# Down weights of the experts: from the sync engine's DMA queue to ACT's, in a two-layer mixer and MoE kernel

## The reference

```python
N_EXPERTS, TOP_K, D_EXPERT = 64, 8, 256
...
    def expert_block(args):
        b_tok, b_w, e = args
        xb = xt[b_tok]
        h = jax.nn.silu(xb @ w_gate[e]) * (xb @ w_up[e])
        return (h @ w_down[e]) * b_w[:, None].astype(xt.dtype)
...
    routed = jax.ops.segment_sum(y_rows.reshape(rows, d), row_tok, num_segments=t)
    shared = (jax.nn.silu(xt @ sw_gate) * (xt @ sw_up)) @ sw_down
    return (routed + shared).reshape(bsz, s, d)
```

## Time and profile before

| | |
|---|---|
| time, 3 runs | 1300.17 us median (1300.01 to 1300.87) |
| the profiled execution | 1300.64 us, of which the span from first to last instruction is 1298.9 us |
| mean granted TensorE clock | 0.997 of full speed |
| PE busy | 1281.4 us, 99% of the span |
| DVE, ACT, POOL busy | 529.0, 190.6 and 46.6 us |
| moved by DMA | 462.33 MB, 356 GB/s over the span |
| expert loads | 128 each of gate, up and down, 1024 KB each |

### The profile page before, as it was taken

One profiled execution on the slowest core, in us unless ns is written; L12 is line 12 of the kernel. 1 busy time (PEld: TensorE's weight loads), 2 busy tenths in 40 slices (PEclk: granted clock), 3 DMA queues, 4 the chain that ended last, 5 costly groups with the idle time before them and its releaser, 6 DMA issues.

```text
span 1298.9 us, 17051 instructions
## 1 busy us (share of the span) xinstructions
PE 1281.4 (99%) x6781; PEld 695.3 (54%) x6781; DVE 529.0 (41%) x1070; ACT 190.6 (15%) x318; POOL 46.6 (4%) x76
## 2 busy tenths in 40 slices
PE   9999999999999999999999999999999999999997
PEld 7874754544445444455487757444544445544443
DVE  6785723333333333333327155333333333333324
ACT  3231201111111111111022303111111111111111
POOL 6200100000000000000010001000000000000000
PEclk9999999999999999999999999999999999999999
DMA  7865959999999999999843278799999999999992
GB/s 256 242 248 191 423 213 412 418 422 422 422 422 421 422 422 422 421 422 421 349 161 130 83 285 337 283 419 420 422 422 422 422 422 422 422 422 422 422 420 87
DMA packets 77625, 462.33 MB, mean 356 GB/s; under 512 B 9680, under 2 KB 10896, under 8 KB 27152
## 3 DMA queue, kind: packets, MB, share of 16 engines
q1 hardware_dynamic: 77584, 461.74, 87.6%
HBM read 455.36 MB, written 6.36 MB: 355 GB/s over the span
## 4 chain that ended last, share of the span: by engine, by line
PE 96%; DVE 2%; DMA 1%; ACT 0%; issue 0%; SPq 0%; ACTq 0%
PE bank L1065 34%; PE bank L1097 18%; PE bank L995 10%; PE bank L1016 9%; PE bank L622 6%; PE bank L636 4%; PE bank L968 2%; PE bank L689 2%; PE bank L703 2%; PE bank L1076 1%; PE bank L1004 1%; PE bank L1030 1%; DMA weight_ring<-in_w_in_even 1%; PE bank L800 1%; DVE h L1353 1%; PE bank L891 1%
## 5 line engine op out<-in xcount | busy, mean ns | idle before, releaser
L1097 PE MATMUL bank<-expert_weights,hiddenT 128*64 128x512 f32 x1024 | 233.8, 598 | 0.0
L1065 PE MATMUL bank<-expert_weights,hT 128*64 128x512 f32 x1024 | 225.3, 592 | 0.0
L1065 PE MATMUL bank<-expert_weights,weight_ring 128*64 128x512 f32 x1024 | 225.2, 592 | 0.0
L1856 DVE TENSOR_TENSOR hidden<-silu_gate,bank 128x256 f32<-128x256 f32 x64 | 27.0, 422 | 330.0 <-ACT silu_gate L1294 330.0
L1065 PEld LDWEIGHTS bank<-expert_weights,weight_ring 128*64 128x64 f32 x1024 | 73.6, 137 | 146.2 <-issue 146.2
L1065 PEld LDWEIGHTS bank<-expert_weights,hT 128*64 128x64 f32 x1024 | 73.4, 137 | 145.3 <-issue 145.0
L1097 PEld LDWEIGHTS bank<-expert_weights,hiddenT 128*64 128x64 f32 x1024 | 67.8, 136 | 118.6 <-issue 110.0
L1016 PE MATMUL bank<-onehot_r,h_top 128*128 128x256 f32 x512 | 128.5, 291 | 0.0
L1016 PE MATMUL bank<-onehot_r,h_low 128*128 128x256 f32 x512 | 123.3, 281 | 0.0
L995 PE MATMUL bank<-y_top,onehotT_r 128*128 128x512 f32 x264 | 112.9, 428 | 0.0
L995 PE MATMUL bank<-y_low,onehotT_r 128*128 128x512 f32 x264 | 105.0, 398 | 0.0
(11 more groups left out here) (361 smaller groups left out, 1070.5 us busy)
## 6 DMA issues: line engine op xcount, KB each, us to landing
expert_weights<-in_exp_w_gate SPq DMA_DIRECT2D x128, 1024.0 KB, 9.9
expert_weights<-in_exp_w_up SPq DMA_DIRECT2D x128, 1024.0 KB, 12.0
expert_weights<-in_exp_w_down SPq DMA_DIRECT2D x128, 1024.0 KB, 11.5
weight_ring<-in_w_in_even SPq DMA_DIRECT2D x6, 2048.0 KB, 10.1
weight_ring<-in_w_out SPq DMA_DIRECT2D x4, 2048.0 KB, 7.5
weight_ring<-in_w_in_odd SPq DMA_DIRECT2D x4, 2048.0 KB, 10.5
s_c<-expert_weights SPq DMA_DIRECT2D x1, 3072.0 KB, 11.6
expert_weights<-s_c SPq DMA_DIRECT2D x1, 3072.0 KB, 11.8
```

The costliest lines, as they stand in the source:

```text
L1065: last_mm = nc.tensor.matmul(bank[6][a * CAP:(a + 1) * CAP, :].rearrange("p (w f) -> p w f", w=2), xq[:, c, s0:s0 + CAP], ew_gu(2 * u + a, c),
L1097: last_mm = nc.tensor.matmul(bank[b][a * CAP:(a + 1) * CAP, :], hm[:, j, a * CAP:(a + 1) * CAP], ew_d(2 * u + a)[:, j, half * 512:(half + ...
L1856: nc.vector.tensor_tensor(hslot[:, :], sg[:, :], bank[6][:, DE:2 * DE], ALU.mult)\
```

## The change

The two down loads of a pair no longer come from SP but from ACT, which issues them directly behind its own L1298, that is behind the same wait on `y_hi_full`. Gate and up loads stay with SP, whose loop over the groups now waits on `gu_full` alone. `first_load` stays with SP; in a second or later pass (which does not run here) SP would also load the down weights of the first group. Both queues feed the same slots and semaphores as before. The last two pairs of a layer issue nothing, as nothing is to be refilled. The line numbers of the changed kernel are some lines higher: the down load is L300, SiLU L1298, the copy L1290 and the high part of the output L1302.

```diff
--- before.py
+++ after.py
@@ -295,8 +295,10 @@
             sp.dma_start(ew[:, s, 0:EW], src_g).then_inc(m["gu_in"][s], 16)
             sp.dma_start(ew[:, s, EW:2 * EW], src_u).then_inc(m["gu_in"][s], 16)
 
-        def down_src(l, e):
-            return A["exp_w_down"][l, e].rearrange("(p j) n -> p (j n)", j=JE)
+        def down_load(eng, m, l, e, s):
+
+            eng.dma_start(ew[:, s, 2 * EW:3 * EW], A["exp_w_down"][l, e].rearrange("(p j) n -> p (j n)", j=JE))\
+               .then_inc(m["d_in"][s], 16)
 
         def sp_ln_params(sp, k, w, b):
             if k:
@@ -360,7 +362,7 @@
 
         def first_load(sp, m, l, s):
             expert_load(sp, m, l, s, s)
-            sp.dma_start(ew[:, s, 2 * EW:3 * EW], down_src(l, s)).then_inc(m["d_in"][s], 16)
+            down_load(sp, m, l, s, s)
 
         EARLY_SLOTS = (2, 3)
 
@@ -385,16 +387,17 @@
                 first_load(sp, m, l, s)
             sp_ln_params(sp, k, A["ln2_w"][l], A["ln2_b"][l])
 
-            def group(base, it):
+            def group(base, it, opening=False):
 
                 for u in range(2):
 
                     sp.wait_ge(m["gu_full"], (base - 1) * 2 + u + 1)
                     for s in (2 * u, 2 * u + 1):
                         expert_load(sp, m, l, it * NSLOT + s, s)
-                    sp.wait_ge(m["y_hi_full"], (base - 1) * 2 + u + 1)
-                    for s in (2 * u, 2 * u + 1):
-                        sp.dma_start(ew[:, s, 2 * EW:3 * EW], down_src(l, it * NSLOT + s)).then_inc(m["d_in"][s], 16)
+                    if opening:
+                        sp.wait_ge(m["y_hi_full"], (base - 1) * 2 + u + 1)
+                        for s in (2 * u, 2 * u + 1):
+                            down_load(sp, m, l, s, s)
 
             with sp.Fori(1, NE // NSLOT) as it:
                 group(it, it)
@@ -402,7 +405,8 @@
             npass = sp.value_load(npass_i[0:1, 0:1], min_val=1, max_val=MAX_PASS)
             with sp.If(npass > 1):
                 with sp.Fori(1, npass) as ps:
-                    with sp.Fori(0, NE // NSLOT) as it:
+                    group(ps * (NE // NSLOT), 0, opening=True)
+                    with sp.Fori(1, NE // NSLOT) as it:
                         group(ps * (NE // NSLOT) + it, it)
             return npass
 
@@ -1297,6 +1301,9 @@
                         act.wait_ge(m["y_hi_full"], n + 1)
                         nc.scalar.activation(y_top[:, 512:1024], bank[5][:, :], ACT.Copy, scale=slot_gate[:, u:u + 1])\
                           .then_inc(m["y_hi"], 1)
+                        if not (last and v == 1):
+                            for s in (2 * u, 2 * u + 1):
+                                down_load(act, m, l, it * 2 * NSLOT + NSLOT * v + NSLOT + s, s)
 
             with act.Fori(0, npass) as ps:
                 gathered(0, 0, ps * PAIRS + 1)
```

## The result

| | before | after |
|---|---|---|
| median | 1299.96 us | 1303.53 us |
| lowest and highest of 11 runs | 1298.49 to 1300.87 | 1300.00 to 1306.75 |
| ratio after to before | | 1.0031, 95% interval 1.0021 to 1.0040 |
| the profiled execution | 1300.64 us | 1300.00 us |
| its span | 1298.9 us | 1298.3 us |

The changed kernel is slower by 3.6 us, 0.3%, and its runs are spread over 6.8 us instead of 2.4. The profiled execution of the changed kernel happens to be its shortest, as short as that of the kernel before; so a comparison of the two totals would show nothing, and the profile has to be read stage by stage. Three more profiles of the changed kernel and two more of the one before were taken for that.

What follows compares the result with a forecast made beforehand. PE was taken to bound the kernel, with DMA just behind. Stalls of 1.0 and 1.3 us gave 2.3 us, 1302.9 us on the profiled execution, so 1302.5 us for the median; range 1299.9 to 1307 us.

Steps and rivals of the forecast that it cites:

- What bounds the kernel: Expert pairs: PE sets the pace at 14.86 us; DMA lags 0.08 us per pair, hidden only by slack before PE.
- SP and ACT: Issuing engines: SP's freed issue time worth 0; ACT's two added issues per pair, 0.81 us of 6.2 us spare, cost 0.
- The transfers: Two queues share the engines, so down loads delay the last up load of a pair, between 0 and 4.98 us.
- my term: Delay taken for the last up load of a pair: all 4.98 us, two down loads of 2.10 MB at 421 GB/s.
- 7.0 us: Last pair of layer 0: transfer the last up load still had ahead when the down loads are issued at 619.85.
- The rate doesn't fall: Rival, both layers: two queues lower the DMA rate, each 1% costing 4.3 us a layer, 1311 us; chance 0.22.
- All hidden: Rival: engines take older loads first or two queues raise the rate, so no stall, 1300.2 us; chance 0.29.
- ACT was not held: Rival: two issues on ACT taking over 6 us would delay the SiLU of 60 pairs; chance 0.03.
- The sum: PE stalls before the last pair, 1.0 us in layer 0 and 1.3 us in layer 1: 2.3 us.
- the slack: Last pair of a layer: time from last up load's landing to PE's need, 4.0 us in layer 0, 3.7 in layer 1.
- The pair before it just holds: Layer 1, last pair but one: with the delay its load lands at 1257.9 against a need at 1258.35, no stall.
- What I said the profile would show: Landing near 20 us at a layer's end, PE idle about 1 us, mid-layer pairs 14.86 us, SiLU on time.

Runs made afterwards that it cites:

- Experiment 3: Changed kernel, but each down load from ACT brings only 512 KB instead of 1024: 1300.05 us, ratio 0.9999.
- Experiments 2: Changed kernel, but the down loads of the last four experts of each layer are back on SP: 1299.95 us, ratio 1.0002.
- experiment 4: Kernel before, one queue, with the next mixer's 2 MB of ring weights issued ahead of layer 0's last gate and up loads: 1302.53 us, ratio 1.0021.
- experiment 5: Changed kernel, with the next mixer's 2 MB of ring weights also issued ahead of layer 0's last gate and up loads: 1311.12 us, ratio 1.0090.

## Why the prediction was right, and what was too small

**What bounds the kernel.** Right: PE by its own work, with DMA slightly too slow and the backlog eating the slack. Experiment 3 shows the other side: with less to load nothing else changes.

**SP and ACT.** Right at 0 for both. Experiments 2 and 3 keep the issues on ACT and lose nothing. The down loads leave ACT a little earlier than I had put them, together with L1302. The ring weights, now issued before the last down loads, did no harm.

**The transfers.** The mechanism is shown. The loss goes when 8 of 120 loads go back behind the last gate and up loads (2), comes with one queue alone when 2 MB are put ahead of them (4), and the stall grows to 6 us when it is done twice (5). That the engines serve both queues without regard to age is seen in the bytes above, 2.08 MB of the younger loads against 1.66 MB of the older in 9 us, and in the landings: over four profiles the last up load of layer 0 landed 19.5, 20.2, 20.6 and 21.2 us after its issue, 20.4 in the mean, against 15.2, 15.8 and 15.5 before, and in layer 1 20.02 against 15.16. That is 4.9 us later in both; my term was 4.98. There was some luck in it. The full 4.98 us are lost only if at least as much of the older loads is left when the down loads begin to move, and I had counted on 7.0 us. They begin 3.4 us after their issue, at what would be 623.3 in the profile of before, and there the last up load landed at 628.7: at most 5.4 us were left. In the changed kernel the last bytes of the down loads moved only 0.5 to 2.0 us before the last up load landed. With a smaller backlog the delay was below my term, as the early pairs show (last paragraph of this section). The rule of the Trainium skill (DMA: Bandwidth & Descriptors, Queues, rings and completion order), round robin between the queues, gives what was seen here; the runs show the shared progress and its nearly even split, not its grain.

**The rivals.** The rate doesn't fall: 421 and 422 GB/s with two queues, as with one. (This rival would have decided from 0.035% on, 0.3 of 8.6 us per percent, not from 0.05%.) The growth of the time to landing, 0.12 to 0.16 us per pair against 0.08 before, is not a lower rate. The even sharing would give it, since with more backlog more of the older loads is left when the down loads begin to move; no run tests this by itself. "All hidden" was true of none of the four profiles of the changed kernel, though of one with the change in layer 0 alone. ACT was not held. The rule that several issuing engines save only issue time (the Trainium skill, DMA: Bandwidth & Descriptors, Issuing engines are not separate DMA queues) holds for the bandwidth, but not for the time of this kernel, since the order of landing changed.

**The sum.** This is the step that was mis-sized: "1.0 + 1.3 = 2.3 us". Measured in four profiles: 1.4, 2.8, 3.1 and 3.4 us; by layer 1.2 and 1.5 us in the mean. Two things were missing. PE doesn't start when the load has landed but about 0.13 us later (landed 630.68, started 630.82 in the first profile), once in each layer: 0.3 us that the sum left out. And the slack was taken from a single execution, 4.0 and 3.7 us, while the landings of layer 0 before differ by 0.6 us from one execution to the next (15.2 to 15.8, 15.5 in the mean); while there is slack such a difference costs nothing, once it is used up it moves the time, up or down. "The pair before it just holds", said of layer 1, was right in two of four, and the misses cost 0.15 us at most; in layer 0 it waited 0.3 us in one of four. So the loss came out at 3.6 us where I had 2.3, inside the range to 1307 but above the 2.6 us that I had called no change. The stalls explain 2.7 us of it in the mean, the lower end of the interval of the loss (1.0021, 2.7 us). The profiled executions are 3.1 us apart, and there the slow stretch at 785 us, 1.6 us in one of four, gives 0.4 more. The other 0.5 us of the timed loss no profile shows; it is well within the interval and may be chance. Whether the change makes the stretch at 785 us more frequent stays open. The wider spread of the changed kernel fits with stalls that differ by 2 us from run to run and with none to three slow stretches in a run, where the three profiles of before have one each.

**What I said the profile would show.** Nearly 20 us to landing, PE idle before the last pair (0.4 to 1.8 us where I had about 1), pairs of 14.86 us in between, the next SiLU on time, a third of the expert bytes on the second queue: all seen. The early up loads are late by less, as I had said: about 225 us they land after 15.2 us in the first profile and 16.7 to 17.8 in the other three, against 13.1 to 13.7 before.

## What to carry to other kernels

A second queue gave its transfers half of the engines from 3.4 us after their issue on, whatever stood in the first. With the DMA engines full (421 GB/s), the loads in the first queue then landed later by what got in between, here 4.9 us for 2 MB. Before a load is moved to another queue, look for the transfer with the least slack at the end of a stage, not at the mean, and add the size of what can now overtake it. Loads that are needed late can stay in the queue of those that are needed soon, and behind them; if the issuing engine is needed for another reason, the last group alone can go back, which here restored the time.

## What I had not expected of the hardware

- The transfers of ACT's queue began to move 3.4 us after their issue in all four profiles of the changed kernel; from then on the two queues moved nearly the same number of bytes, whichever was older.
- Issues can become slow: SP's gate and up loads mostly took 0.33 to 0.44 us each, but with 2 MB more in its queue three of four took 1.59, 1.68 and 1.33 us (experiment 4), and in experiment 5 one took 2.33 us. I take this for a wait behind what is outstanding; no run tests it. The loads behind a slow issue are issued later, so their time to landing looks shorter than the delay is.
- After 6 us without work PE ran the next 32 matmuls in 8.93 instead of 7.04 us; the granted clock was 0.52 from 633 to 639 us, across the end of the idle time and the start of the work. After stalls of up to 1.8 us they took 7.09 us. A stall of 6 us cost nearly 8.
- Equal executions of one kernel differ by stretches of lower clock, 0.83 in a window of 10 us, worth 1.6 us at 785 us, that come and go at a few fixed places (near 60, 145 and 785 us).
